# Value pages of a paged latent cache: from 128 rows of one token to 64 rows of two

## The reference, cut to what matters

```python
ckv_past = pool_ckv[layer_idx, page_table].reshape(db, -1, A_KV_LORA)   # 8 x 4096 x 256
kpe_past = pool_kpe[layer_idx, page_table].reshape(db, -1, A_ROPE)      # 8 x 4096 x 32
sc_past = einsum('bshc,btc->bhst', q_lat, ckv_past) + einsum('bshr,btr->bhst', q_pe, kpe_past)
p = softmax(concatenate([sc_past * SM_SCALE, sc_self], axis=-1), axis=-1)
o_lat = einsum('bhst,btc->bshc', p[..., :n_past], ckv_past) + ...
```

## Time and profile before

| | |
|---|---|
| median of 3 runs | 2308.16 us (2303.6 to 2312.53) |
| the profiled execution | 2304.24 us, span 2302.5 us |
| granted clock of TensorE over the span | 0.970 |
| PE, DVE, ACT, POOL busy | 95%, 45%, 33%, 5% of the span |
| scores run | from 571.2 to 842.6 us |
| values run | from 608.4 to 879.9 us |

### The profile page before, as it was taken

How to read it: one execution, slowest core, us unless ns; L and a number is a source line. 1 busy time by engine, 2 the same in 40 slices (tenths; PEclk the granted TensorE clock), 3 DMA queues, 4 the chain that set the end, 5 groups by cost and what they waited for, 6 DMA issues and landing times.

```text
span 2302.5 us, 46795 instructions
## 1 busy us (share of the span) xinstructions
PE 2189.5 (95%) x18285; PEld 2078.3 (90%) x18285; DVE 1033.1 (45%) x1994; ACT 750.2 (33%) x1305; POOL 119.9 (5%) x226
## 2 busy tenths in 40 slices
PE   7999999998777878999999999999999999999997
PEld 7999999997443557999999999999999999999997
DVE  5444344366653343544443444443346664444333
ACT  5222232464222432522222342222232234222222
POOL 0000000001134331000000000000000000000000
PEclk9999999998886897999999999999999999999998
DMA  4222233234799972222223222222322222222231
GB/s 151 91 91 91 91 101 100 83 128 134 210 271 277 248 204 71 92 92 91 91 91 101 101 92 91 91 90 93 99 94 91 91 93 92 91 91 91 92 101 65
DMA packets 100014, 261.98 MB, mean 114 GB/s; under 512 B 14386, under 2 KB 47171, under 8 KB 99843
## 3 DMA queue, kind: packets, MB, share of 16 engines
q1 hardware_dynamic: 88722, 228.83, 31.6%
q0 software_dynamic: 11184, 31.69, 4.7%
HBM read 255.29 MB, written 5.16 MB: 113 GB/s over the span
## 4 chain that ended last, share of the span: by engine, by line
PE 61%; DVE 1%; ACT 1%; issue 0%; DVEq 0%; ACTq 0%
PE bank L276 20%; PE bank L275 20%; PE bank L277 20%; PE bank L1845 0%; PE bank L1828 0%; PE bank L1859 0%; PE bank L1834 0%; ACT sb_prob L826 0%; DVE sb_prob L1314 0%; DVE sb_x L1435 0%; PE bank L1620 0%; PE bank L293 0%; DVE sb_x L362 0%; ACT L301 0%; ACT L298 0%
## 5 line engine op out<-in xcount | busy, mean ns | idle before, releaser
L275 PE MATMUL bank<-sb_h_hi,sb_w_hi 128*128 128x260 f32 x3552 | 1007.3, 284 | 15.2 <-DVE sb_w_lo L252 12.0
L276 PE MATMUL bank<-sb_h_lo,sb_w_hi 128*128 128x260 f32 x3552 | 1007.9, 284 | 0.0
L277 PE MATMUL bank<-sb_h_hi,sb_w_lo 128*128 128x260 f32 x3552 | 1004.6, 283 | 0.0
L246 ACT ACTIVATE sb_w_hi<-sb_raw 128x1024 fp32r<-128x1024 f32 x339 | 359.0, 1060 | 1239.4 <-PE bank L277 1237.7
L275 PEld LDWEIGHTS bank<-sb_h_hi,sb_w_hi 128*128 128x128 f32 x3552 | 669.4, 188 | 17.7 <-DVE sb_w_lo L252 12.0
L277 PEld LDWEIGHTS bank<-sb_h_hi,sb_w_lo 128*128 128x128 f32 x3552 | 672.3, 189 | 0.0
L276 PEld LDWEIGHTS bank<-sb_h_lo,sb_w_hi 128*128 128x128 f32 x3552 | 669.0, 188 | 0.2
L252 DVE TENSOR_TENSOR sb_w_lo<-sb_raw,sb_w_hi 128x1024 fp32r<-128x1024 f32 x339 | 415.0, 1225 | 379.1 <-ACT sb_w_hi L246 378.2
L276 PE MATMUL bank<-sb_a_lo,sb_w_hi 128*128 128x260 f32 x1408 | 399.1, 283 | 0.0
L275 PE MATMUL bank<-sb_a_hi,sb_w_hi 128*128 128x260 f32 x1408 | 398.5, 283 | 0.0
L277 PE MATMUL bank<-sb_a_hi,sb_w_lo 128*128 128x260 f32 x1408 | 397.7, 282 | 0.0
(11 more groups left out here) (262 smaller groups left out, 1576.3 us busy)
## 6 DMA issues: line engine op xcount, KB each, us to landing
sb_raw<-in_w SPq DMA_DIRECT2D x339, 512.0 KB, 3.5
sb_s_raw<-in_cache SPq DMA_DIRECT2D x256, 144.0 KB, 4.9
sb_v_raw<-in_cache POOLq DMA_DIRECT2D x192, 128.0 KB, 5.6
sb_v_raw<-in_cache SPq DMA_DIRECT2D x64, 128.0 KB, 6.1
sb_x<-in_x SPq DMA_DIRECT2D x4, 520.0 KB, 6.3
out_y<-sb_x SPq DMA_DIRECT2D x8, 260.0 KB, 2.2
sb_st<-in_state POOLq DMA_DIRECT2D x8, 256.0 KB, 7.3
out_state_s<-sb_st POOLq DMA_DIRECT2D x8, 256.0 KB, 5.3
```

Source lines behind the costliest of these rows:

```text
L246: nc.scalar.activation(w_hi[slot][:], raw[slot][:], ACT.Copy).then_inc(S("w_hi_done"), 1)
L275: nc.tensor.matmul(out, wh, xh, start=first and c == 0, stop=False)
L276: nc.tensor.matmul(out, wh, xl, start=False, stop=False)
L277: mm = nc.tensor.matmul(out, wl, xh, start=False, stop=last and c == chunks - 1)
```

## The change

The value copy of a page is laid out as 64 rows of two tokens: row r holds token r and token 64 + r, 2 KB together. The two pages of a job go one above the other into the tile, page 0 into partitions 0 to 63 and page 1 into partitions 64 to 127; the tile's size, the bytes and the number of DMAs stay. The score columns of a job are written in the matching order, token half by token half and inside it page by page, so that a transposed piece of 128 columns again matches the partitions of `v_raw`. The multiplications stay the same in number and size; the operand `both` of the score multiplication is read in four runs of 64 numbers for each partition where it was two runs of 128.

```diff
+V_TOK = JOB
+V_ROWS = PAGE // V_TOK
...
-            rows, lo, width = (SR, 0, S_W) if kind == "s" else (PAGE, SR * S_W, KV_LORA)
+            rows, lo, width = (SR, 0, S_W) if kind == "s" else (V_ROWS, SR * S_W, V_TOK * KV_LORA)
             for j in range(JOB):
-                eng.dma_start(slots[k % RING][0:rows, j, :],
-                              dram["cache"][bass.ds(page_numbers[j], 1), lo:lo + rows * width].rearrange("a (p w) -> (a p) w", w=width)) \
+                to = slots[k % RING][0:rows, j, :] if kind == "s" else \
+                    slots[k % RING][j * V_ROWS:(j + 1) * V_ROWS].rearrange("p u c -> p (u c)")
+                eng.dma_start(to, dram["cache"][bass.ds(page_numbers[j], 1), lo:lo + rows * width].rearrange("a (p w) -> (a p) w", w=width)) \
                     .then_inc(loaded(kind, k), 16)
...
-                        out = S_BANK[CG * j:CG * (j + 1), q % 2 * JOB * P:(q % 2 + 1) * JOB * P].rearrange("p (j t) -> p j t", j=JOB)
-                        last = mm(out, q_s[0:SR, i, c, :], s_raw[(COLG * n + j) % RING][0:SR, :, c * P:(c + 1) * P],
+                        out = S_BANK[CG * j:CG * (j + 1), q % 2 * JOB * P:(q % 2 + 1) * JOB * P].rearrange("p (u w r) -> p u w r", u=V_TOK, w=JOB)
+                        both = s_raw[(COLG * n + j) % RING][0:SR, :, c * P:(c + 1) * P].rearrange("p w (u r) -> p u w r", u=V_TOK)
+                        last = mm(out, q_s[0:SR, i, c, :], both,
...
-                for w in range(JOB):
+                for u in range(V_TOK):
                     for j in range(COLG):
-                        at_p = (JOB * q + w) * P + CG * j
-                        last = mm(V_BANK[CG * j:CG * (j + 1), 0:KV_LORA], p_t[:, at_p:at_p + CG], v_raw[(COLG * n + j) % RING][:, w, :],
+                        at_p = (V_TOK * q + u) * P + CG * j
+                        last = mm(V_BANK[CG * j:CG * (j + 1), 0:KV_LORA], p_t[:, at_p:at_p + CG], v_raw[(COLG * n + j) % RING][:, u, :],
...
+    lat = lat.reshape(POOL, V_TOK, V_ROWS, KV_LORA).transpose(0, 2, 1, 3)
     cache = np.concatenate([both.reshape(POOL, -1), lat.reshape(POOL, -1)], axis=1)
```

More of the change, by code:

```diff
@@ L1616, in values @@
                 quad_loaded(pe, "v", n)
-                for w in range(JOB):
+                for u in range(V_TOK):
                     for j in range(COLG):
-                        at_p = (JOB * q + w) * P + CG * j
-                        last = mm(V_BANK[CG * j:CG * (j + 1), 0:KV_LORA], p_t[:, at_p:at_p + CG], v_raw[(COLG * n + j) % RING][:, w, :],
-                                  start=q == 0 and w == 0, stop=q == QUADS - 1 and w == JOB - 1 and j > 0)
+                        at_p = (V_TOK * q + u) * P + CG * j
+                        last = mm(V_BANK[CG * j:CG * (j + 1), 0:KV_LORA], p_t[:, at_p:at_p + CG], v_raw[(COLG * n + j) % RING][:, u, :],
+                                  start=q == 0 and u == 0, stop=q == QUADS - 1 and u == V_TOK - 1 and j > 0)
                 last.then_inc(S("v_done"), 1)
```

## The result

The changed kernel takes 2317.66 us (median of 16 runs, 2312.38 to 2326.25), the kernel before 2305.72 us beside it (16 runs). The ratio is 1.006, with a 95% interval of 1.0049 to 1.007: 12 us by the medians, slower by a little over 0.5%. The prediction was 2330 us. The profiled execution has a span of 2314.5 us, 12.0 more than before.

The account below looks back on a forecast made before the run. It took the middle part to be near balance between page transfers and PE's own chain. The profiled 2304.2 us plus 22 us (17 quads at 1.3) gave 2326, plus 3.9 to the median: 2330 us, range 2302 to 2356.

Parts of the forecast that it names:

- Where it acts, and what costs nothing: Only the middle part, about 560 to 880 us, can change; matrix work and issuing by POOL and SP cost 0.
- Half the partitions is the large term: Value pages landing in 64 partitions slow the loaded stage, up to 2.2 us a quad; longer rows bring only a small gain.
- The price for a quad: In the full stage, each quad of 8 score and 8 value pages costs 1.3 us more, 60% of 2.2.
- the ratio 1.57: w_uk, loaded into 64 partitions, was 1.57 times as slow per engine and byte as value pages over 128; carried to value pages.
- the upper end: 2.2 us a quad in the full stage: 8 value pages at 278 ns more each, as if nothing overlapped.
- the lower end: 0 us a quad: consecutive pages go to opposite halves, and a held engine may serve its other queue.
- Seventeen full quads, the middle eight covered: 17 quads of the recurrence and prompt attention pay 22 us; the 8 between, 700 to 780 us, hide their 10.4 us.
- Faster transfers can return at most 12.0 us: PE waits 7.5 us for score and 4.5 us for value pages; faster transfers can return no more than that sum.
- the faster rival: Longer rows speed up value pages, 0.39 us a quad or 6.6 us in all, at best 2296 us; chance 0.12.
- Full price: Queues hinder each other wholly: 2.2 us on 17 quads, plus some 8 us from the middle window, 2353 us; chance 0.22.
- my case of 22: Likeliest case: 1.3 us a quad on 17 full quads, 22 us more, 2330 us; chance 0.46.
- the absorbed one: Memory ports have room, less than 0.6 us a quad is left: within 10 us, said as 2311 us; chance 0.20.

Follow-up runs that it names:

- the order alone: The changed kernel with the new order of score columns, but value pages loaded as before in 128 rows of 1 KB: 2304.94 us, 0.9999 to the kernel before.
- the two split runs: The changed kernel with narrow (64-row) value pages only for POOL's three jobs of a quad, or only for SP's one: 1.0046 and 1.0025 to the kernel before.
- the spread kernel: The changed kernel with 2 KB rows, page 0 in even and page 1 in odd partitions, score operand read with a step: 2301.8 us, 0.9989 to the kernel before.
- the four wide stretches: Kernels that only move pages: score pages in 96 partitions beside value pages of 128 rows of 1 KB; 262, 275, 270, 282 GB/s.
- the three narrow ones: Kernels that only move pages: score pages in 96 partitions beside value pages of 64 rows of 2 KB in alternating halves; 245, 251, 250 GB/s.
- the second spread one: The changed kernel with pages in even and odd partitions, operand read in runs of 64, output written with a step of two: 2303.22 us, 0.9986 to the kernel before.

## Why the prediction was right, and which term was mis-sized

**Where it acts, and what costs nothing: right.** The stretches outside the middle part are unchanged, both multiplications took 379 ns, and the order alone gave 0.9999. POOL's issue went from 536 to 516 ns, so it cost nothing either. The statement that SP's issue costs nothing was wrong in its number (351 to 473 ns): I took w_uk, which POOL issued, for SP's queue too. What it cost is at most the small part that the two split runs leave open, and the spread kernel, with 480 ns, lost nothing.

**Half the partitions is the large term: right, and shown.** The loss appears with the halves at both row lengths (1.006, 1.0071), is absent with wide pages in the new order (0.9999) and with 2 KB rows spread over all partitions (0.9989), and divides with the pages. What is argued and not shown is the picture of two engines at one entrance: the runs show that the placing over partitions decides, not which entrance each engine used, and the spread pages give the meeting itself no support. The port rule of the page SBUF — State Buffer in the Trainium skill, "Door 1: The DMA port swizzle", fits the 202 GB/s of pages all in the lower half (its 196 for one transfer of 64 partitions). The Trainium skill's same page, "Can I just issue two DMAs to hit both halves?", gives 6% for two transfers into the two halves, and here a stream of pages in alternating halves brought 244 over 202, 21%; for such a stream the measured 21% counts.

**The price for a quad: the step that was mis-sized.** I took 1.3 us, 60% of the 2.2 that follow from the ratio 1.57. With nothing computed, a quad of 2.23 MB takes 8.2 us at the mean of the four wide stretches (262, 275, 270, 282: 272 GB/s) and 9.0 at that of the three narrow ones (245, 251, 250: 249 GB/s), 0.77 us more, a third of the upper end. 17 x 0.77 = 13 us, against 12 measured. Even with all value pages in the lower half (230 GB/s) a quad takes 9.7 us, 1.5 more, so the upper end of 2.2 was not reached in the worst placing. The ratio 1.57 was that of a transfer into one half alone. Value pages by themselves lose 291/202 = 1.44 when all lie in one half, and only 291/244 = 1.19 when they alternate, as the changed kernel's do. That alternation was in the text as a reason for the lower end and got too little weight.

**Seventeen full quads, the middle eight covered: right in the sum.** Three quads' score multiplications start, in the kernel before and then in the changed one, at

```profile
622.99 1.26 PE L1605 MATMUL bank<-sb_s_raw,sb_q_s 96*32 96x256 f32 x20
...
700.79 1.51 PE L1605 MATMUL bank<-sb_s_raw,sb_q_s 96*32 96x256 f32 x12
...
781.50 1.50 PE L1605 MATMUL bank<-sb_s_raw,sb_q_s 96*32 96x256 f32 x24 [0.44 <-ACT sb_s_all L716]
```

```profile
622.71 1.48 PE L1609 MATMUL bank<-sb_s_raw,sb_q_s 96*32 96x256 f32 x24
...
705.47 1.94 PE L1609 MATMUL bank<-sb_s_raw,sb_q_s 96*32 96x256 f32 x16
...
786.72 1.91 PE L1609 MATMUL bank<-sb_s_raw,sb_q_s 96*32 96x256 f32 x22 [2.94 <-DMA sb_s_raw<-in_cache]
```

These are the starts of the eighth, seventeenth and twenty-fifth quad. The nine quads of the recurrence took 82.8 instead of 77.8 us, 0.55 us each; the eight of the middle window 81.3 instead of 80.7, so the cover held; and from there to the last score multiplication 68.6 instead of 61.1 us (855.3 and 842.6 less these starts), 7.5 over eight quads or so. The seventeen together cost 12.5 us, 0.73 each. At the windows' own rates (269 to 247, 263 to 237 GB/s) the transfers of a quad grow by 0.74 us in the recurrence and by 0.93 in the prompt's attention. The latter is paid in full. In the recurrence a quad took 8.6 us before and its transfers 8.3, so part of the growth found room; which of PE's other waits gave it is not shown.

**"Faster transfers can return at most 12.0 us": wrong, though it moved no number of the forecast beyond the faster rival.** Score pages in 128 partitions returned 18.7 us by the ratio (0.81% of 2306) and 20.9 by the medians. The middle part, from 560 to 905 us in the kernel before (its row is above), ends at 884 in that one:

```profile
560.00:884.00 324.00, 255.04 (x2391) 156.95 (x2392) 159.83 (x486) 95.24 (x252) 110.94 (x205) 0.85 0.75 236
```

PE's idle time there fell from 78.9 to 69.0 us, which is within the bound of 12.0. The other 11.0 us are busy time, 255.0 for 266.1 us with the same multiplications, at a mean granted clock of 0.85 for 0.82. So the bound left out that PE's work itself can get shorter. How much of the 11.0 us the transfers brought stays open: these are single executions, and the busy time of the middle part is 270.0 us in the order-only kernel and 259.6 in the second spread one.

**The rivals.** Full price (2353) and faster (2296) are out. The measured 12 to 14 us lie between my case of 22 and the absorbed one of at most 10. In the changed kernel the longer rows brought nothing that can be seen, as the sum had it.

## What to carry to other kernels

Where transfers set the pace, look at which partitions each lands in before you look at the length of its rows: 64 rows in one half of the partitions lost 8 to 10% of the rate beside another stream (269 to 247 and 263 to 237 GB/s here, 272 to 249 with nothing computed), and the same rows in every second partition lost nothing. To price a shape, take a row in which it runs as it will run in the kernel; a ratio from a transfer alone in one half gave a price almost three times too high (2.2 for 0.77 us a quad) for pages that alternate between halves. A list of direct waits is no upper bound for what faster transfers can return: when they returned some 20 us here, half of it was PE's busy time and not its waiting.

## What the runs showed of the hardware that I had not expected

Score pages in 96 partitions, beside wide value pages, hold the whole stream at 262 to 282 GB/s; the same bytes in 128 rows of 1152 bytes give 343 to 348, and 0.8% of this kernel. By themselves the two shapes differ only by 5% (281 and 295). SP's time to issue one DMA depends on its shape: 351 ns for a value page in 128 rows, 473 in 64 rows of 2 KB, 608 in 64 rows of two pieces. A float32 operand read with an innermost step of 384 numbers, from one page of a job to the other, took the multiplication from 379 to 437 ns, while writing the output with a step of two numbers left it at 379.
